# Attention of a two-network forward pass: two narrow items of a head become one, and the last dilated head gets an order of its own

## What is computed

```python
def mla_attention(q_nope, q_rope, k_nope, k_rope, v):
    ...
    def block(qs):                        # Q_BLOCK = 128 queries
        qn, qr = qs
        s = (jnp.einsum('bqhd,bkhd->bhqk', qn, k_nope)
             + jnp.einsum('bqhr,bkr->bhqk', qr, k_rope))
        prob = jax.nn.softmax(s.astype(jnp.float32) * scale, axis=-1).astype(v.dtype)
        return jnp.einsum('bhqk,bkhd->bqhd', prob, v)
...
        att_x = mla_attention(qn_x, qr_x, concatenate([kn_x, kn_c]), ...)   # 512 queries, 768 keys, 8 heads
...
        if not last:
            att_c = mla_attention(qn_c, qr_c, kn_c, kr_c, v_c)              # 256 queries, 256 keys, 8 heads
```

## Time and profile before

| | |
|---|---|
| runs | 3 |
| median (lowest to highest) | 3460.04 us (3453.33 to 3461.95) |
| the profiled execution's own time | 3459.95 us |
| its span in the trace | 3458.2 us |
| mean granted TensorE clock | 0.982 of full |
| busy share: TensorE, VectorE, ScalarE, GpSimd | 95%, 58%, 38%, 2% |
| DMA | 356 MB moved, 103 GB/s mean |

### The profile page before, as it was taken

One profiled execution on the slowest core, in us unless ns is written; L12 is line 12 of the kernel. 1 busy time (PEld: TensorE's weight loads), 2 busy tenths in 40 slices (PEclk: granted clock), 3 DMA queues, 4 the chain that ended last, 5 costly groups with the idle time before them and its releaser, 6 DMA issues.

```text
span 3458.2 us, 42699 instructions
## 1 busy us (share of the span) xinstructions
PE 3289.7 (95%) x17650; PEld 2713.6 (78%) x17650; DVE 1999.6 (58%) x2797; ACT 1314.1 (38%) x1949; POOL 56.7 (2%) x59
## 2 busy tenths in 40 slices
PE   7898999999999999999989999999899999889998
PEld 3685568888888755988887888888888888788887
DVE  6677676777556476565557655333655555563333
ACT  3323455132234245533354544222533333362223
POOL 0000000000000000000000010000100000020000
PEclk8999999999999999999999999999999999999999
DMA  5542022545443310355522212323143233223221
GB/s 177 167 128 68 13 80 93 158 152 159 153 152 125 99 64 25 126 183 183 183 73 75 74 62 86 110 98 98 53 99 80 68 94 77 59 81 103 98 98 49
DMA packets 375408, 356.13 MB, mean 103 GB/s; under 512 B 73471, under 2 KB 320558, under 8 KB 373807
## 3 DMA queue, kind: packets, MB, share of 16 engines
q1 hardware_dynamic: 374995, 353.32, 33.5%
q10 hardware_dynamic: 220, 0.07, 0.0%
HBM read 345.50 MB, written 4.72 MB: 101 GB/s over the span
## 4 chain that ended last, share of the span: by engine, by line
PE 50%; DVE 5%; ACT 3%; issue 1%; POOL 0%; DMA 0%; SPq 0%; DVEq 0%; ACTq 0%; POOLq 0%
PE ps L414 45%; PE ps L2818 1%; DVE r_st L2701 1%; PE ps L2839 1%; PE ps L2828 1%; DVE second_w_lo L582 1%; ACT second_scr L733 1%; ACT second_w_hi L522 1%; DVE x_res L917 1%; DVE second_scr L915 0%; PE ps L2841 0%; DVE sums L498 0%; DVE second_scr L744 0%; PE ps L2547 0%; PE ps L2553 0%
## 5 line engine op out<-in xcount | busy, mean ns | idle before, releaser
L414 PE MATMUL ps<-second_h_hi,second_w_hi 128*128 128x512 f32 (+1 forms) x2216 | 819.0, 370 | 45.4 <-DVE second_h_lo L943 25.1
L414 PE MATMUL ps<-second_h_hi,second_w_lo 128*128 128x512 f32 (+1 forms) x2216 | 806.2, 364 | 0.0
L414 PE MATMUL ps<-second_h_lo,second_w_hi 128*128 128x512 f32 (+1 forms) x2216 | 805.4, 363 | 0.0
L582 DVE TENSOR_TENSOR second_w_lo<-ring,second_w_hi 128x2048 fp32r<-128x2048 f32 (+2 forms) x175 | 371.5, 2123 | 458.3 <-ACT second_w_hi L522 458.2
L414 PEld LDWEIGHTS ps<-second_h_hi,second_w_hi 128*128 128x128 f32 x2216 | 423.7, 191 | 112.4 <-issue 29.8
L414 PEld LDWEIGHTS ps<-second_h_hi,second_w_lo 128*128 128x128 f32 x2216 | 423.5, 191 | 65.7
L414 PEld LDWEIGHTS ps<-second_h_lo,second_w_hi 128*128 128x128 f32 x2216 | 423.9, 191 | 61.1
L522 ACT ACTIVATE second_w_hi<-ring 128x2048 fp32r<-128x2048 f32 (+2 forms) x175 | 310.0, 1771 | 273.4 <-PE ps L414 264.1
L414 PE MATMUL ps<-h_mix_hi,w_mix_hi 128*128 128x512 f32 (+2 forms) x776 | 268.8, 346 | 8.4 <-DVE w_mix_lo L582 4.3
L414 PE MATMUL ps<-h_mix_lo,w_mix_hi 128*128 128x512 f32 (+2 forms) x776 | 266.5, 343 | 0.0
L414 PE MATMUL ps<-h_mix_hi,w_mix_lo 128*128 128x512 f32 (+2 forms) x776 | 266.1, 343 | 0.0
(11 more groups left out here) (461 smaller groups left out, 5396.4 us busy)
## 6 DMA issues: line engine op xcount, KB each, us to landing
ring<-in_w_mlp SPq DMA_DIRECT2D x64, 1024.0 KB, 5.3
side_w<-in_ada_w SPq DMA_DIRECT2D x96, 512.0 KB, 5.0
ring<-in_ffn_w_in SPq DMA_DIRECT2D x44, 1024.0 KB, 5.0
side_w<-in_w_mod SPq DMA_DIRECT2D x80, 512.0 KB, 3.8
ring<-in_attn_w_in SPq DMA_DIRECT2D x48, 512.0 KB, 5.3
ring<-in_hgrn_w_in SPq DMA_DIRECT2D x32, 512.0 KB, 4.8
ring<-in_ffn_w_out SPq DMA_DIRECT2D x16, 1024.0 KB, 5.0
ring<-in_w_in SPq DMA_DIRECT2D x14, 1024.0 KB, 5.6
```

Source lines behind the costliest of these rows:

```text
L414: mm = pe.matmul(acc, lhsT, rhs, start=at == 0 and wp == ap, stop=at == j.kt - 1 and wp == 1)
L582: dve.tensor_tensor(unit.place(unit.slot[1]), unit.place(M.ring[:, u % RING, :]), unit.place(unit.slot[0]), ALU.subtract).then_inc(*S.w_lo ...
```

## The change

**Narrow units.** The two items of a narrow unit become one: the scores of both blocks of 128 queries stand side by side in one pair of banks, one reduce gives both row maxima, two exponentials and two scalings follow as before, four transposes as one turn and one copy of them. `nmax`, `esum` and `rsum` get eight columns for it, and the recurrence's Ln and Exp name four of them. A head of the first layer has five items in place of six. The steps keep their distance in items, save that values come three items behind the last of their unit, and `at()` follows `pace`, in which the merged item has the middle of the two old places. The half copy and the store have a new place where a narrow unit follows. The second layer has no narrow units.

**The last dilated head** gets its own class with places for scores, turns and values, and orders on ScalarE and VectorE written out. It also takes over the split of `second_y`, and VectorE's low part of the output projection's second weight unit is issued in it.

```diff
@@ HeadThread.freed
-            eng.wait_ge(X.S.scores.sem, X.S.scores.at(2 * X.per_head * (self.head - 1)))
+            eng.wait_ge(X.S.scores.sem, X.S.scores.at(X.items_per_head * (self.head - 1)))
@@ AttendThread
-        self.n_items, self.y_bank = 2 * len(self.units), []
+        for u, (_, _, _, w) in enumerate(self.units):
+            self.begun.append(len(self.items))
+            if w == T:
+                self.items += [(u, (0,)), (u, (1,))]
+                self.pace += [2 * u, 2 * u + 1]
+            else:
+                self.items.append((u, (0, 1)))
+                self.pace.append(2 * u + 0.5)
+            self.ended.append(len(self.items) - 1)
+        self.n_items, self.y_bank = len(self.items), []
+        self.pace += [self.pace[-1] + 1 + i for i in range(4)]
...
     def at(self, n, inside):
-        return self.start + n * self.width / 2 + inside
+        return self.start + self.pace[n] * self.width / 2 + inside
...
+        for m, i in enumerate(parts):
+            a = 0
+            while a < w:
+                at = n % 2 * 1024 + m * w + a
...
@@ AttendThread.tensor
-            if n >= 4 and n % 2 == 0:
-                self.values(pe, n // 2 - 2)
+            if n - 3 in self.ended:
+                self.values(pe, self.ended.index(n - 3))
@@ AttendThread.exponent
-        act.activation(M.f[:, n % 2, 0:w], self.item(n), ACT.Exp, bias=M.nmax[:, n % 4:n % 4 + 1],
-                       accum_out=M.esum[:, n % 4:n % 4 + 1]).then_inc(*S.exped.one)
+        for m in range(len(self.items[n][1])):
+            a, c = self.part(n, m)
+            e = act.activation(M.f[:, n % 2, a], self.item(n)[:, a], ACT.Exp, bias=M.nmax[:, c], accum_out=M.esum[:, c])
+        e.then_inc(*S.exped.one)
@@ AttendThread.scalar
-            if n >= 4 and n % 2 == 0:
-                yield self.at(n, 4.8)
-                self.other_half(act, n // 2 - 2)
+            if n - 3 in self.ended:
+                u = self.ended.index(n - 3)
+                yield self.at(n, 3.2 if self.narrow_next(u) else 4.8)
+                self.other_half(act, u)
@@ AttendThread.maximum
+        x, c = self.item(n), self.cols(n)
+        if len(self.items[n][1]) == 2:
+            x = x.rearrange("p (i k) -> p i k", i=2)
+        dve.tensor_reduce(M.nmax[:, c], x, AX, ALU.max, negate=True).then_inc(*S.maxed.one)
@@ Region.vector
-                self.low(dve, u)
+                if self.units[u] not in self.later:
+                    self.low(dve, u)
@@ new
+class LastDilatedThread(DilatedThread):
+    SCORES_AT, TURN_AT, VALUES_AT = (0.0, 0.001, 0.477, 0.525), (0.476, 0.524, 0.62, 0.668), (0.523, 0.573, 0.667, 0.715)
...
+        steps = sorted([(at, 2, u) for u, at in enumerate(self.SCORES_AT)] + [(at, 0, u) for u, at in enumerate(self.TURN_AT)] +
+                       [(at, 1, u) for u, at in enumerate(self.VALUES_AT)])
...
+    def block_high(self, act, k):
+        S, M = self.S, self.M
+        act.wait_ge(S.stored.sem, S.stored.at(k + 1))
...
+        for k in range(KD - 1):
+            self.block_high(act, k)
+        self.exponent(act, 0)
+        self.exponent(act, 1)
+        self.keep(act, 0)
+        self.keep(act, 1)
+        self.exponent(act, 2)
+        self.exponent(act, 3)
+        self.keep(act, 2)
+        self.keep(act, 3)
+        self.block_high(act, KD - 1)
...
+    def vector(self, dve):
+        S, M, n = self.S, self.M, self.n
+        yield self.end
+        self.mask(dve, 0)
+        for k in range(KD - 1):
+            self.block_low(dve, k)
+        self.mask(dve, 1)
+        self.normalise(dve, 0)
+        self.normalise(dve, 1)
+        self.mask(dve, 2)
+        self.mask(dve, 3)
+        self.normalise(dve, 2)
+        self.normalise(dve, 3)
+        self.R.low(dve, self.low_unit.u)
...
+        self.block_low(dve, KD - 1)
@@ dilated
-            last.append(SplitThread(R, [(b, M.y[:, b, :]) for b in range(KD - 1)], h, 0, LX, ends[-1],
-                                    [(S.stored, H2 - 1), (S.acc, ends[-1] + 1)]))
...
+        thread = DilatedThread(R, B, n, ends, k_jobs, following) if following else \
+            LastDilatedThread(R, B, n, ends, k_jobs, h, out_unit)
```

More of the change, by code:

```diff
@@ L312, in __init__ @@
         self.held, self.slot_turn = {}, -1
-        self.group_of = {}
+        self.group_of, self.later = {}, set()
         self.count = {"act": 0, "dve": 0}
@@ L1364, in __init__ @@
         self.per_head = 2 if self.last else 3
+        self.items_per_head = 4 if self.last else 5
         def sb(name, shape, kb):
@@ L1802, in item, with cols, part @@
         return self.X.flat[:, at:at + self.wide(n)]
+    def cols(self, n):
+        at = 2 * (n % 4)
+        return slice(at, at + len(self.items[n][1]))
+    def part(self, n, i):
+        w, at = self.keys(n), 2 * (n % 4) + i
+        return slice(i * w, (i + 1) * w), slice(at, at + 1)
     def scores(self, pe, n):
         X, S = self.X, self.X.S
-        u, i = n // 2, n % 2
+        u, parts = self.items[n]
         h, q0, k0, w = self.units[u]
@@ L1841, in values @@
         h, _, k0, w = self.units[u]
[L1842 removed]
+        pe.wait_ge(S.probs_t.sem, S.probs_t.at(self.ended[u] + 1))
         bank = X.banks.oldest(self.Y_BANKS)
@@ L1861, in tensor @@
                 self.turn(pe, n - 2)
-            if n >= 4 and n % 2 == 0:
-                self.values(pe, n // 2 - 2)
+            if n - 3 in self.ended:
+                self.values(pe, self.ended.index(n - 3))
     def keep(self, act, n):
-        X, S, w = self.X, self.X.S, self.wide(n)
-        u, i = n // 2, n % 2
+        X, S, w = self.X, self.X.S, self.keys(n)
+        u, parts = self.items[n]
+        i, k = parts[0], len(parts)
         act.wait_ge(S.turned.sem, S.turned.at(n + 1))
@@ L1913, in maximum @@
             dve.wait_ge(S.probs.sem, S.probs.at(n - 3))
-        dve.tensor_reduce(M.nmax[:, n % 4:n % 4 + 1], self.item(n), AX, ALU.max, negate=True)\
-            .then_inc(*S.maxed.one)
+        x, c = self.item(n), self.cols(n)
+        if len(self.items[n][1]) == 2:
+            x = x.rearrange("p (i k) -> p i k", i=2)
+        dve.tensor_reduce(M.nmax[:, c], x, AX, ALU.max, negate=True).then_inc(*S.maxed.one)
     def normalise(self, dve, n):
-        S, M, w = self.X.S, self.X.M, self.wide(n)
+        S, M, c = self.X.S, self.X.M, self.cols(n)
         dve.wait_ge(S.exped.sem, S.exped.at(n + 1))
-        dve.reciprocal(M.rsum[:, n % 4:n % 4 + 1], M.esum[:, n % 4:n % 4 + 1]).then_inc(*S.recip.one)
+        dve.reciprocal(M.rsum[:, c], M.esum[:, c]).then_inc(*S.recip.one)
         dve.wait_ge(S.recip.sem, S.recip.at(n + 1))
-        dve.tensor_scalar(M.f[:, n % 2, 0:w], M.f[:, n % 2, 0:w], M.rsum[:, n % 4:n % 4 + 1], None,
-                          ALU.mult).then_inc(*S.probs.one)
+        for m in range(len(self.items[n][1])):
+            a, c = self.part(n, m)
+            o = dve.tensor_scalar(M.f[:, n % 2, a], M.f[:, n % 2, a], M.rsum[:, c], None, ALU.mult)
+        o.then_inc(*S.probs.one)
     def store(self, dve, u):
@@ L1937, in vector @@
                 self.normalise(dve, n - 1)
-            if n >= 4 and n % 2 == 0:
-                yield self.at(n, 5)
-                self.store(dve, n // 2 - 2)
+            if n - 3 in self.ended:
+                u = self.ended.index(n - 3)
+                yield self.at(n, 3.4 if self.narrow_next(u) else 5)
+                self.store(dve, u)
 class HyenaThread(Thread):
@@ L2589, in mean_root @@
         act.wait_ge(S["rec_ln"].sem, S["rec_ln"].at(n + 1))
-        act.activation(M.rsum[:, :], M.rsum[:, :], ACT.Exp, scale=-0.5).then_inc(*S["rec_rstd"].one)
+        act.activation(M.rsum[:, 0:4], M.rsum[:, 0:4], ACT.Exp, scale=-0.5).then_inc(*S["rec_rstd"].one)
     def high_part(self, act, n):
@@ L3032, in dilated @@
             R.sides.append(NormaliseThread(thread))
-    last.append(SplitThread(R, [(KD - 1, M.y[:, KD - 1, :])], h, 0, LX, ends[-1], [(S.stored, H2)]))
-    return {**last[0].needs(), **last[1].needs()}
+    return thread.needs()
 FFN_PARTS = ((0, 3), (3, 4), (7, 4))
@@ L3180, in second_network @@
     TableThread(R, D_.masks[:, :], io["attn_masks"], R.jobs[-1].at + 2 * N_LATE + 2)
-    ready = dilated(R, io, h, D_, normed)
+    out_units = square_cuts(io["attn_w_out_2"][0])
+    ready = dilated(R, io, h, D_, normed, out_units[1])
     R.slots, R.slot_turn = slots, -1
-    out = output(1, square_cuts(io["attn_w_out_2"][0]), h, ready, (0, 1, 2))
+    out = output(1, out_units, h, ready, (0, 1, 2))
     borders = ffn(1, out)
```

115 lines of the change are left out of this document (94 added, 21 removed).

## The result

The changed kernel takes 3470.62 us (median of 8 runs, 3469.0 to 3481.33), the kernel before in the same comparison 3458.49 us (8 runs, 3453.33 to 3461.95). The ratio is 1.0041, with a 95% interval from 1.0032 to 1.0050: slower by 0.41%, some 14 us by the ratio and 12 by the medians. The profiled execution took 3469.38 us, its span is 3467.6 us, at a mean granted clock of 0.981.

The account below looks back on a forecast made before the run. TensorE, busy in 95% of the span, was taken as the bound, so only its idle time and clock counted. Attention +8.6 (11.6 - 3.0) and last head -3 gave +5.6 on 3459.95: 3465.5 us, range 3448 to 3480.

Parts of the forecast that it names:

- no change, on the slow side: Whole kernel: 3465.5 us, within the 10.4 us a measurement can tell; the forecast with its spread, 3461 to 3470, had 0.39.
- Heads 0 to 3, +11.6: First layer's attention: Hyena groups and projections directly behind the values wait for the store; 2.9 us lost in each head.
- The first bound: Heads 0 to 3: only the Hyena group's wait for the store counts, 0.9 us each, +3.6 in all.
- Heads 4 to 7, -2.5: First layer's attention: longer merged scores cover part of the wait before the first unit's turn; -1.7 to -4.3, taken as -2.5.
- the tail, -0.5: End of the attention stage: one item less saves an estimated 0.5 us, about one narrow item's scores.
- the relief of VectorE: Attention stage: merging saves VectorE some 2.5 us over eight heads; costed at nothing because TensorE's matmuls cover it.
- The last head, -3: Last dilated head: earlier mask and removed turn wait against a new low-weights wait; between -1.3 (sure) and -4.5 (upper bound).
- The rule: Skill text on operation size, for the attention stage: grouping would gain 2.5 us if VectorE were saturated; otherwise the stage loses.
- Half clock spreading: Rival, chance 0.27: new waits bring half clock in heads 0, 2 and 3, losing 12 us: 3477.
- The faster rival: Rival, chance 0.16: waits before turns shrink by 6, head 1's half clock goes (-3), last head gains 4.5: 3446.5 us.
- nothing on the path: Rival, chance 0.13: attention's loss and gain cancel, last head's moved weights give back the masks' gain; within 3 us of 3460.
- the last head turning the wrong way: Rival, chance 0.05: moved low weights hold TensorE 2.9 us, the ring's load comes late, head ends 2 us later: 3470.5.

Follow-up runs that it names:

- everything together: The whole change plus the Hyena groups' offset of 4.5, the mixer's low weights moved, the output unit's low weights in VectorE's hole: 3456.61 us for 3459.52, ratio 0.9995.

## Why the prediction was right or wrong

The time lies in the range, and the side was right, but the change costs 12 to 14 us for the 5.6 forecast, and so more than the 10.4 us that I had called measurable. Most likely was "no change, on the slow side"; what came is just beyond. The range held it because it was wide: the stage lost 15.2 us for the 8.6 forecast, and only the last head's larger gain (4.7 for 3) took some of that back.

*Heads 0 to 3, +11.6: right in size and mechanism, with some luck head by head.* 12.5 measured, by the mechanism named. In head 0 the idle time ahead of the group was foretold at 2.1 us and is 1.95; the projection comes 23.15 us after the stage's first scores before and 25.80 after, +2.65 for the +2.9 walked. Head 1 was short: 3.9 for 2.8. The group itself came only 0.5 later against head 0's projection (the 0.75 of the walk), but behind the turn's wait of 2.67 us the values ran at half clock, 2.83 us for 1.5. Head 2 gave only 0.75 and head 3 5.2, so "2.9 for each" was right as a mean alone. Head 2's 0.75 hides a wait of 2.94 us: in the kernel before, its stretch began with a projection at half clock (5.49 us at 346.23), and that went. The first bound, that only the first wait counts (+3.6), is refuted by the turn that waits 2.33 us in head 0.

*Heads 4 to 7, -2.5, and the tail, -0.5: wrong, and this is the term that failed.* Heads 4 and 5 gained 0.6, heads 6 and 7 lost 3.2: +2.6 in place of -3.0. The merged scores do cover 0.43 us more (the turn that waited 1.07 us at 434.84 waits 0.64). But the merged item also asks VectorE for 0.68 + 0.70 us ahead of its own turn, and in heads 6 and 7 two of these turns wait long: 2.10 us at 489.03, and 3.09 at 472.86 behind the mixer's low weights, with 2.74 us at half clock for 1.5 behind it. Heads 4 to 7 were to show no more than short waits. I had set the relief of VectorE at nothing "because TensorE covers it" and forgot to ask what the longer item costs where TensorE has nothing to cover it with. I had also not looked at that low part, which the new time stamps put ahead of a reduce. How much each of the two carries is not shown: undone one at a time, they gave back 0.6 and 0.4 of the 3.2 us.

*The last head, -3: right in its steps, small in its sum.* First product -1.3 (1.5 measured), no wait at the first turn, 2.9 us for low weights (2.52 measured). In the head 4.7 of 41.0 us went, near the full-clock bound of 4.5, since the clock rose from 0.92 to 0.95. In the kernel with the last head alone it was 1.00, behind the same wait for low weights, and 6.2 went; the merged item in front is not the reason, for with everything together it was 1.00 too.

*The rule.* The Trainium skill's "Perfetto Trace Analysis", section "Optimizing Scalar/DVE Operations", says that where VectorE is not saturated but causes bubbles, breaking instructions up may let work finish sooner. The end of the stage agrees, weakly: the last narrow unit in two items again gave 0.6 us back. The kernel that moves only the places loses 13.0 us in the stage, some 11 of them in heads 0 to 3, without any larger operation, so there it is the order and not the size.

*The rivals.* Half clock spreading: the time is near what it asked for, its mechanism is not what happened. The clock of heads 0 to 3 is 0.94 for 0.95, and 14 of 15 us are idle time. Head by head it was 1.00, 0.93, 0.90 and 1.00 before and is 1.00, 0.90, 1.00 and 0.89 now: of the heads 0, 2 and 3 that the rival named, head 3 alone fell below 0.9. What was held against the rival, that waits of about 1 us brought no half clock, was true of the kernel before behind 401 us and not in its head 1: see the last section. The faster rival, nothing on the path, and the last head turning the wrong way are refuted by the stretches above.

## What to carry to other kernels

A step placed by a time stamp is placed against others: when a table of items is made shorter, look through all threads for what has slipped behind the one that frees its buffer, and print the order on each engine. A shared bank costs little as long as two pieces of other work lie between its last use and the next claim, here 0 to 1.0 us; taken directly behind the use, it costs the way through the other engines, here 0.9 to 3.5 us each time. Before putting an operation at the end of an engine's list "out of the way", look for idle time of that engine in the middle: the same low part of the weights cost a wait of 2.5 us at the end of the list, and in a hole of 3.8 us the head was 2.0 us shorter.

## What was not expected of the hardware

Two exponentials back to back, each with its read of the row sum, start 0.47 us apart (305.02 and 305.49), while the time from one to ScalarE's next instruction of another kind is 0.58 us: the second costs less than the 0.59 us that I had added for it. Half clock does not follow a wait by its length alone, and not even the same wait in the same code. The kernel before has one in head 1 that none of its rows showed, and the kernel with the last head and the low weights in the hole has the same attention:

```profile
346.23 5.49 PE L1696 MATMUL ps<-p,mx_wq 128*128 128x512 f32 x6 [0.99 <-DVE p L1929]
```

```profile
346.78 2.84 PE L1697 MATMUL ps<-p,mx_wq 128*128 128x512 f32 x6 [0.99 <-DVE p L1930]
```

The turn just before had waited 1.20 us in both. Waits of 0.99 and 1.20 us were thus followed by half clock in one trace and by full clock in the other; in a third, that of the last head alone, the projection behind waits of 0.91 and 0.99 us took 4.54. The same holds for longer waits: behind 1.95 us in head 0 the group took 1.99 us in the changed kernel and 3.16 in the one with the merged item alone; behind 2.77 us in the kernel with the groups moved back, the projection took 5.49 us in head 0 and 2.84 in head 1. A single place of half clock in one trace is therefore no ground for a price.
